# Reordering the turn from the output projection to the experts in a one-core hybrid decoder step

## The reference, cut to what matters

```
x = x + merged @ w_out
xt = rmsnorm(x) * norm2_g
g_logits = xt @ w_rg + b_rg ;  e_logits = xt @ w_rexp + b_rexp
one group of 4 (top 1), then 2 of its 8 experts (top 2), weights w
for e in range(32):
    h = silu(xt @ w_e_gate[e]) * (xt @ w_e_up[e])       # 1024 -> 256
    y = y + combine[:, e:e+1] * (h @ w_e_down[e])       # 256 -> 1024
out = rmsnorm(x + y) * final_norm_g
```

## Time and profile before

| | us |
|---|---|
| median of 3 runs | 782.0 (781.23 to 782.25) |
| the profiled execution's own time | 780.97 |
| its span | 779.2 |
| TensorE busy | 736.3 (94%) |
| VectorE busy | 409.2 (53%) |
| ScalarE busy | 260.4 (33%) |
| data moved | 190.78 MB, mean 245 GB/s |

### The profile page before, as it was taken

How to read it: one execution, slowest core, us unless ns; L and a number is a source line. 1 busy time by engine, 2 the same in 40 slices (tenths; PEclk the granted TensorE clock), 3 DMA queues, 4 the chain that set the end, 5 groups by cost and what they waited for, 6 DMA issues and landing times.

```text
span 779.2 us, 12795 instructions
## 1 busy us (share of the span) xinstructions
PE 736.3 (94%) x5298; PEld 569.7 (73%) x5298; DVE 409.2 (53%) x756; ACT 260.4 (33%) x451; POOL 74.8 (10%) x105
## 2 busy tenths in 40 slices
PE   8999999999999999999999999998899999778784
PEld 6999999999999777899999988884333333323232
DVE  6989839996347685666154286555121121114226
ACT  5652351123476636443243333230111111100113
POOL 0100022001002111000000100011111212111100
PEclk9999999999999999999999999999999999999999
DMA  8578326434338442500251596289999999999994
GB/s 342 204 261 323 109 82 91 132 115 146 110 114 307 161 176 87 214 1 1 109 180 51 186 396 265 89 352 385 416 423 423 418 424 423 421 424 424 422 400 185
DMA packets 38191, 190.78 MB, mean 245 GB/s; under 512 B 5930, under 2 KB 7498, under 8 KB 21912
## 3 DMA queue, kind: packets, MB, share of 16 engines
q1 hardware_dynamic: 23696, 148.22, 48.1%
q0 software_dynamic: 11248, 35.08, 13.4%
q10 hardware_dynamic: 3184, 6.60, 2.3%
HBM read 176.27 MB, written 21.41 MB: 254 GB/s over the span
## 4 chain that ended last, share of the span: by engine, by line
PE 76%; DMA 14%; DVE 5%; ACT 3%; issue 1%; SPq 1%; DVEq 0%; ACTq 0%; POOLq 0%
PE ps L667 72%; DMA sb<-in_wexp 11%; PE ps L681 4%; DMA expert_rows<-sb 2%; DMA sb<-expert_rows 1%; DVE sb L2799 1%; DMA sb<-in_xT 1%; DVE sb L2330 1%; DVE sb L2316 1%; SPq L567 1%; ACT sb L1455 1%; ACT sb L1655 1%; DVE sb L2732 0%; ACT sb L1677 0%; ACT sb L1660 0%
## 5 line engine op out<-in xcount | busy, mean ns | idle before, releaser
L667 PE MATMUL ps<-sr 128*128 128x288 f32 (+3 forms) x2906 | 407.3, 300 | 3.5 <-DVE ps L2737 3.1
L667 PEld LDWEIGHTS ps<-sr 128*128 128x128 f32 (+1 forms) x2906 | 386.7, 188 | 18.9 <-issue 5.8
L667 PE MATMUL ps<-sb 128*64 128x512 f32 (+17 forms) x1994 | 292.5, 427 | 28.6 <-DMA sb<-in_wexp 16.5
L667 PEld LDWEIGHTS ps<-sb 128*64 128x64 f32 (+7 forms) x1994 | 143.1, 146 | 150.5 <-issue 123.4
L2666 DVE SCALAR_TENSOR_TENSOR sb<-sb,ps 128x256 f32<-128x256 f32 x16 | 6.7, 421 | 117.5 <-ACT sb L1860 117.5
L681 PEld LDWEIGHTS ps<-sb 128*128 128x128 f32 (+3 forms) x398 | 42.2, 140 | 32.6 <-issue 30.2
L681 PE MATMUL ps<-sb 128*128 128x128 f32 (+3 forms) x398 | 53.7, 273 | 3.8 <-DVE sb L2669 1.6
L2278 DVE TENSOR_TENSOR sr<-sb,sr 128x2048 fp32r<-128x2048 f32 (+1 forms) x17 | 39.3, 2319 | 29.0 <-ACT sr L1569 19.0
L2674 DVE COPY sb<-ps 128x1024 f32<-128x1024 f32 x15 | 18.4, 1225 | 56.1 <-PE ps L667 56.1
L1455 ACT ACTIVATE sb<-ps 128x576 f32<-128x576 f32 (+4 forms) x33 | 23.2, 704 | 71.8 <-PE ps L667 56.0
L2389 DVE SCALAR_TENSOR_TENSOR sb<-sb,ps 128x576 f32<-128x576 f32 x24 | 18.1, 753 | 46.5 <-PE ps L667 46.3
(11 more groups left out here) (293 smaller groups left out, 499.7 us busy)
## 6 DMA issues: line engine op xcount, KB each, us to landing
sb<-in_wexp SPq DMA_DIRECT2D x91, 1024.0 KB, 21.9
sb<-in_wstream SPq DMA_DIRECT2D x33, 1024.0 KB, 6.1
expert_rows<-sb ACTq DMA_DIRECT2D x1, 4608.0 KB, 24.9
sb<-in_mkT POOLq DMA_DIRECT2D x8, 512.0 KB, 6.9
sb<-in_mv POOLq DMA_DIRECT2D x8, 512.0 KB, 5.1
sb<-expert_rows SPq DMA_DIRECT2D x4, 1024.0 KB, 9.5
sb<-in_wexp SPq DMA_DIRECT2D x5, 768.0 KB, 23.3
sb<-in_x SPq DMA_DIRECT2D x4, 512.0 KB, 14.2
```

The source lines that it names most:

```text
L667: return signed(nc.tensor.matmul(*a, **kw))
```

## The change

It changes the order of work in the turn, not what is computed.

- The `w_out` jobs run as w02, w22, w03, w04, w23, w24. Slots 10 to 13 of the ring now lie on blocks 0 and 1 and are issued when w04 is filled, slot 14 when w23 is, slots 15 to 18 when w24 is.
- Tiles 3 and 4 are turned, squared and multiplied with the router in two column halves (jobs xa and xb; the mean square is made of two sums, the first passed as bias to the root).
- The gain `norm2_g` is no longer in the normalized rows: ScalarE writes them as a scaled copy (`scaled_rows`), and VectorE applies the gain at each pair's turn, in two halves (`rows_turned`, `turned_half`), in place of ScalarE's one copy. VectorE's `norm` and GpSimd's multiply are gone, and so is the load of the gain for all partitions (512 KB).
- The constant of `ranks` carries -2048 on its diagonal, so that one comparison tells both that a row chose an expert and where it goes: `select_first` takes 2 operations on the PSUM result in place of 3 that came behind `place_rows`.
- The second column half of `first_rows(4)` and the expert counts move behind `gate_up(0, 0)`; the 19 small VectorE operations that make numbers and gate weights move behind `rows_turned(1)`, and ScalarE's two Exp behind the first pair's tanh.
- PSUM tiles from w03 on are given by a table written by hand (`plan_pairs`).

```diff
+SLOTS_E += [straight(24320), straight(O_A + 16640)]
+SLOTS_E += w_out_slots(0)
+SLOTS_E += [[(27648, ((1280, 2), (1, 1024)), 0, 2048)]]
+SLOTS_E += w_out_slots(2)
...
-            for n, job in ((8, "w31"), (9, "w22"), (10, "w23")):
+            for n, job in ((8, "w31"), (9, "w22")):
                 filled(sp, job)
                 main_chunk(n)
-            sp.wait_ge(w_used, NBLOCKS - 2)
-            for n in range(11, 15):
+            filled(sp, "w04")
+            for n in range(10, 14):
                 main_chunk(n)
-            sp.wait_ge(w_used, NBLOCKS)
+            filled(sp, "w23")
+            main_chunk(14)
+            filled(sp, "w24")
             for n in range(15, 19):
...
TensorE, from tile 3 on:
+            two_blocks(0, 3, range(5))
+            turn_h("x2T2", 2, all_kts)
+            two_blocks(0, 3, range(5, KT))
+            table(1)
+            logits(2, "x2T2", all_kts)
+            two_blocks(0, 4, range(1))
+            logit_sums(2)
+            two_blocks(0, 4, range(1, 4))
+            turn_h("xa3", 3, low_half)
+            two_blocks(0, 4, range(4, 7))
+            ranks(2)
+            two_blocks(0, 4, range(7, KT))
+            two_blocks(2, 3, range(3))
+            table(2)
+            turn_h("xa4", 4, low_half)
+            two_blocks(2, 3, range(3, 6))
+            logits(3, "xa3", low_half)
+            two_blocks(2, 3, range(6, KT))
+            two_blocks(2, 4, range(2))
+            turn_h("xb3", 3, high_half)
+            two_blocks(2, 4, range(2, 4))
+            logits(3, "xb3", high_half)
+            two_blocks(2, 4, range(4, 5))
+            logit_sums(3)
+            logits(4, "xa4", low_half)
+            two_blocks(2, 4, range(5, KT))
+            first_rows(0, low_half)
+            ranks(3)
+            turn_h("xb4", 4, high_half)
+            first_rows(1, low_half)
+            first_rows(2, range(2))
+            logits(4, "xb4", high_half)
+            first_rows(2, range(2, 4))
+            logit_sums(4)
+            first_rows(3, low_half)
+            first_rows(0, high_half)
+            first_rows(1, high_half)
+            table(3)
+            ranks(4)
+            first_rows(2, high_half)
+            first_rows(4, low_half)
+            table(4)
+            first_rows(3, high_half)
...
                 gate_up(i, 0)
                 if i == 0:
+                    first_rows(4, high_half)
+                    counts()
...
                 gate_up(i, 1)
...
ScalarE:
+            def first_square(t):
+                act.wait_ge(h_ready, first_h(t))
+                square(t, 0, D // 2, R_SA + t)
+                part = at(R_SA + t, (1, 1), pn=WROWS[t])
+                fn(part, part, ACT.Identity, scale=1.0 / D, bias=at(O_EPS, (1, 1), pn=WROWS[t])).then_inc(half_root, 1)
...
+            copy_turned("x2T2", 2, range(KT))
+            first_square(3)
+            copy_logits(2)
+            scaled_rows(2)
+            copy_turned("xa3", 3, low_half)
+            first_square(4)
+            copy_turned("xa4", 4, low_half)
+            for t in (3, 4):
+                second_square(t)
+                copy_turned(f"xb{t}", t, high_half)
+                copy_logits(t)
+                scaled_rows(t)
...
VectorE:
+                filled(dve, f"rk{t}")
+                op(v.tensor_tensor(at(sel, (RB, 2), (1, RB), pn=R), at(R_ROW, (0, 2), (1, RB), pn=R),
+                                   pat(pair(f"rk{t}"), 0, (1, 2), (0, RB), pn=R), ALU.is_equal))
+                c.do(v.tensor_scalar(at(sel, (1, 128), pn=R), at(sel, (1, 128), pn=R), at(R_SS + t, (1, 1), pn=R), None, ALU.mult),
                      sel0_ready)
...
+            def rows_turned(i):
+                dve.wait_ge(xt_ps, i + 1)
+                wait_pos(dve, gu_ps, i)
+                turned_half(PS_X, 0).then_inc(half_sb, 1)
+                turned_half(PS_X, 1).then_inc(xT_sb, 1)
...
+            add_h(0, 4)
+            add_table(2)
+            add_h(2, 3)
+            inverse_norm(3)
+            choose(3)
+            add_h(2, 4)
+            select_first(3)
+            place_rows(3)
             inverse_norm(4)
             choose(4)
+            select_first(4)
+            place_rows(4)
             add_table(3)
-            place_rows(4)
-            select_first(4)
-            first_turned()
+            first_turned(0)
             add_table(4)
             dve.sem_inc(idx_ready, 1)
+            first_turned(1)
...
                 for i in range(i0, i1 - 1):
                     hidden(i)
                     if i == i0:
                         result(i)
+                    rows_turned(i + 1)
+                    if i == 0:
+                        numbers_and_gates()
```

More of the change, by code:

```diff
@@ L37 @@
 NOROW = 4096
+CHOSEN = 2048
 WB = 2048
@@ L283, in plan_jobs @@
     jobs += pieces_at(n + 1)
[L284 to L290, removed]
+    jobs += ["w00", "w20", "w01", "w11", "x2T0", "w21", "lT0", "lg0", "w31"]
+    jobs += ["rk0", "x2T1", "w02", "tb0", "lT1", "lg1", "w22"]
+    jobs += ["rk1", "x2T2", "w03", "tb1", "lT2", "lg2", "xa3", "rk2", "w04"]
+    jobs += ["tb2", "xa4", "w23", "xb3", "lT3", "lg3", "w24"]
+    jobs += ["rk3", "xb4", "lT4", "lg4", "tb3", "rk4", "xs", "tb4", "cnt"]
     return {j: i for i, j in enumerate(jobs)}
@@ L372, with plan_pairs @@
 J = plan_jobs()
-PS_X, PS_GU, PS_H, PS_Y = (J[job] % 4 for job in ("tb4", "rk4", "cnt", "xs2"))
+def plan_pairs():
+    pairs = {job: i % 4 for job, i in J.items() if i <= J["lg2"]}
+    p0, p1, p2, p3 = (pairs[job] for job in ("lT2", "lg2", "w03", "tb1"))
+    assert sorted((p0, p1, p2, p3)) == list(range(4))
+    pairs.update(w04=p2, xa3=p3, rk2=p0, w23=p1, tb2=p0, xa4=p3, lT3=p2, w24=p0, xb3=p1, lg3=p1, lT4=p3)
+    pairs.update(rk3=p1, xb4=p0, xs=p2, lg4=p0, tb3=p1, rk4=p0, tb4=p1, cnt=p3)
+    return pairs
+PAIR = plan_pairs()
+NTH = {job: sum(PAIR[other] == PAIR[job] for other in J if J[other] < J[job]) for job in J}
+TURNED = ["x2T0", "x2T1", "x2T2", "xa3", "xa4", "xb3", "xb4"]
+PS_X, PS_GU, PS_H, PS_Y = (PAIR[job] for job in ("tb4", "rk4", "cnt", "xs"))
 SEEDED = {1: PS_GU, 3: PS_Y, 4: PS_GU}
@@ new lines, in _ @@
+            low_half, high_half = range(4), range(4, KT)
+            all_kts = range(KT)
+            one_block(0)
+            one_block(1)
+            turn_h("x2T0", 0, all_kts)
+            one_block(2)
+            logits(0, "x2T0", all_kts)
+            one_block(3, range(3))
+            logit_sums(0)
+            one_block(3, range(3, KT))
+            two_blocks(0, 2, range(2))
+            ranks(0)
+            two_blocks(0, 2, range(2, 5))
+            turn_h("x2T1", 1, all_kts)
+            two_blocks(0, 2, range(5, KT))
@@ new lines, in _ @@
+            table(0)
+            logits(1, "x2T1", all_kts)
+            two_blocks(2, 2, range(1))
+            logit_sums(1)
+            two_blocks(2, 2, range(1, KT))
+            ranks(1)
+            two_blocks(0, 3, range(5))
[7 more added lines that the diff above has]
+            turn_h("xa3", 3, low_half)
@@ L1314, in body @@
                 gate_up(i, 1)
+                if i == 0:
+                    for ps_ in (PS_X, PS_H, PS_Y):
+                        emptied(ps_)
                 if last:
@@ L1871, in pairs @@
                         hidden_turned(i)
-                    if i < i1 - 1:
-                        rows_turned(i + 1)
+                    if i == 0:
+                        gates()
                 hidden_turned(i1 - 1)
```

342 lines of the change are left out of this document (164 added, 178 removed).

## The result

| | before | after |
|---|---|---|
| median of 22 runs, us | 781.44 | 783.33 |
| lowest and highest, us | 779.6, 783.89 | 781.66, 785.99 |
| ratio, 95% interval | | 1.0020 [1.0012, 1.0029] |
| profiled execution, us (span) | 780.97 (779.2) | 783.52 (781.7) |

The change makes the kernel about 1.6 us slower (0.0020 x 781.4; the medians lie 1.9 us apart), which lies on the bound of 0.2%. I had forecast 782.1 us against 782.0, that is +0.1. The time lies in the whole range, 780.4 to 784.2, but above my forecast's own range of 781.4 to 783.0; the size was wrong by 1.5 us.

The account below looks back on a forecast made before the run. From 557 us the weight stream bounds it, so when it last runs dry decides. Chunk 19 and chunks 22 and 23 allowed -0.2 to +0.6, taken as +0.1: 781.1 us profiled, plus 1.0 gives 782.1; range 780.4 to 784.2.

Parts of the forecast that it names:

- rival 3: Turn: tile 4's chain, `add_h(2, 4)` behind all of `choose(3)`, is late and delays the first pair; 783.9 us, chance 0.15.
- At what time does the weight stream last run dry: Weight stream in the turn: the deciding question; before, it would have run dry at 544.4 us, 1.4 us to spare.
- I credit 0 for it by itself: Early chunks in slots 10 to 13: they fill 3.7 us of idle DMA time but only empty the queue sooner; 0.
- rival 1: Early chunks: the 3.7 us of filled idle DMA time carries through to the end; 778.3 us, chance 0.09.
- rival 2: Turn: rows land 1 to 2 us earlier, `gate_up(0, 1)` no later; 780.6, at most 780.1 us; chance 0.09.
- Plus 0.3 for three more pieces: TensorE before `gate_up(0, 0)`: three more pieces of turns and logits start anew, 0.1 us each, bounds 0 to 0.2.
- The last rows go out about 0.6 us later: ScalarE scales the last rows behind tile 4's logits copy; landing for chunk 19 between 0.4 earlier and 0.6 later.
- I take +0.1, near the middle of what both sides allow: Stream's resumption: the later of chunk 19 and chunks 22 and 23 moves it -0.2 to +0.6 us; taken as +0.1.
- `choose(4)` 524.4 to 524.8: Start of `choose(4)` in the turn: no earlier than its 524.49 before, as its shorter chain begins behind all of `choose(3)`.
- Moving numbers and gates "gives nothing": VectorE's 19 operations, 5.0 us, move from before the first pair's tanh to about 549 to 554 us; cost 0.
- Identity at nothing: ScalarE's new `first_square`: Identity between Square and Sqrt needs no table loads, 0; other bound two loads a tile, 2.56 us.
- The wait of 0.35 us at 499: TensorE waits for the copy of tile 2's logits, as ScalarE has `first_square(3)` ahead of it; plus 0.35 us.

Follow-up runs that it names:

- late_chunks: Changed kernel with chunks 10 to 13 waiting for w23 in place of w04; 785.07 us, ratio 1.0052 to the kernel before.
- merged: Changed kernel with the router's low halves of tiles 3 and 4 multiplied directly ahead of the high ones, two pieces fewer; 783.07 us, ratio 1.0014.
- release: Changed kernel with chunks 22 and 23 issued at the end of `gate_up(0, 1)`, not at the first instruction behind it; 782.47 us, ratio 1.0016.
- scaled_first: Changed kernel with ScalarE scaling tile 4's rows ahead of the copy of its logits; 783.66 us, ratio 1.0024.
- numbers_ahead: Changed kernel with numbers and gates ahead of the first pair again, on VectorE and ScalarE; 784.11 us, ratio 1.0028.
- rows_ahead: Changed kernel with the high half of `first_rows(4)` back ahead of `gate_up(0, 0)`, the counts staying behind it; 782.46 us, ratio 1.0013.
- three_edits: Changed kernel with `first_rows(4)`'s high half ahead of `gate_up(0, 0)`, 22 and 23 issued at `gate_up(0, 1)`'s end, router halves set together; 782.34 us, ratio 1.0001.
- merged_release: Changed kernel with the router's halves set together and chunks 22 and 23 issued at the end of `gate_up(0, 1)`; 782.21 us, ratio 1.0014.

## Why the prediction was right about the mechanism and wrong in size

The number is inside the range partly by luck. The range reached up to 784.2 us for the sake of rival 3, whose cause did not act in the changed kernel (below), and by a sign that I had set myself, "a second dip near 544", the forecast of +0.1 was wrong: the dip came, 342 GB/s at a share of 0.91 from 544 to 546 us.

- **"At what time does the weight stream last run dry"** was the right question. late_chunks shows it with an unchanged TensorE, and from 557 us on the changed kernel streams at 423 GB/s with TensorE idle for 1.04 us of 79, which costs nothing.
- **"I credit 0 for it by itself"**, the early chunks: right as a forecast of the change, since rival 1 and rival 2 did not come. But they are not worthless: without them the changed kernel is 1.7 us slower (stream: 1.7). They help to make up for 15 to 18, which go 1.6 us later than before (520.29 against 518.71). I had moved 15 to 18 back by 1.1 and never priced that.
- **"Plus 0.3 for three more pieces"** is the term that was mis-sized on TensorE's side. merged measures 0.3 us a piece, above the upper bound. 15 to 18 were already 0.5 late, and `gate_up(0, 0)`, which I put at 531.5, began at 538.19 - 2.2 - 3.5 = 532.5 (20 and 21, which its end releases, went at 536.20 against 536.15): the 0.9 us that the reordering was to give did not come. The starts of TensorE's matmuls from `table(1)` (497.07 before, 496.69 after) to `gate_up(0, 0)` say where it went. The way takes 0.43 us longer, where my terms make it 0.92 shorter. The work that left saves 1.2 us. The 72 matmuls of 512 columns on it take 17.35 us before and 18.14 after, the 48 of the logits 2.95 and 3.37, the three sums and four tables 1.63 and 2.06: 1.6 us more for the same matmuls, now in more pieces. The wait at 499 us is 0.34 of that, so the pieces cost 1.3 us in place of 0.3. From there my own arithmetic holds. The added wait, foreseen as 2.15 us, is 2.2: VectorE's second half goes at 537.29 and TensorE begins at 538.19. So `gate_up(0, 1)` was at 538.19 in place of 537.1, and 22 and 23 at 543.66 in place of 542.6. I had written that each us counts from 537.3 on, which gives 0.9. The dip itself, by the windows and by release, costs 0.3 to 0.4.
- **"The last rows go out about 0.6 us later"**: they went out 1.2 us later. GpSimd's issue was at 525.13 before and at 526.32 after, since ScalarE's scaling began at 523.68 and 524.86:

```profile
523.68 1.15 ACT L1841 ACTIVATE sb<-sb 128x1024 f32<-128x1024 f32 x1 [0.18 <-DVE sb L2491]
```

```profile
524.41 0.28 ACT L1539 ACTIVATE sb<-ps 128x128 f32<-128x128 f32 x1 [1.40 <-PE ps L698]
524.86 1.15 ACT L1937 ACTIVATE sb<-sb 128x1024 f32<-128x1024 f32 x1 [0.17 <-ACT sb L1539]
```

  Before, the scaling waited for VectorE's inverse; after, it stands behind the copy of the logits, for which ScalarE was idle for 1.40 us. The landing was 0.8 us shorter (8.0 in place of 8.8 us, GpSimd's issue to chunk 19's), as foreseen of an emptier queue. So chunk 19 was 0.42 us later, inside my -0.4 to +0.6.
- **"I take +0.1, near the middle of what both sides allow"** is the step that failed. The side of 22 and 23: bytes 1.6 us behind the issue at 543.66, at 545.3, against the 544.4 at which the stream was to run dry, +0.9. The side of chunk 19: +0.42. Both have 0.36 more, since this execution ran 0.36 us ahead at the last issue from `in_wstream`: 1.3 and 0.8 us. Both came out late at once, because both hang on the time at which TensorE is done with tile 4 (its logits for the rows, the first pair behind them for 22 and 23); I had taken a middle value as if one could make up for the other. It is also why the single edits bring so little: mend one side, and the other is left (release: 1.5 of delay; scaled_first: 1.2). In bytes of all queues, 13.53 MB had moved between 504.4 and 543 us before and 13.23 after, 0.7 us; the dip from 543 to 547.5 adds 0.36. Another 0.4 us (0.18 MB) is lost at 552 to 557 us, at a share of 0.99 but 365 in place of 400 GB/s; why the engines move less there at nearly the same share I did not find out, and no run tells it. The sum is 1.5 us.
- **"`choose(4)` 524.4 to 524.8"**: it began at 525.32 (rival 3's chain of tile 4, 0.8 late, with the pieces ahead of it). Rival 3 decides "from `gate_up(0, 1)` at 537.3 on" and gives 782.0 + (538.19 - 537.3) = 782.9 for what came, 0.4 below what was measured. So the rival's arithmetic held, but not its cause. VectorE's `choose(3)` ended as w24 was done (15 to 18, which wait for it, went at 520.29), so that `add_h(2, 4)` ran from 520.50 to 521.18 with next to no wait, and TensorE turned tile 4's high half only at 521.74. In merged, where w24 is done 1.05 us sooner behind w04, that chain does hold TensorE up, by 0.3 us.
- **Moving numbers and gates "gives nothing"**: they ran from 550.25 to 555.1 us, ahead of `hidden(1)` at 557.42, as foreseen. But numbers_ahead shows that leaving them where they were would have cost 0.9 us of stream. The cost of 0 held only against the kernel before.
- **Identity at nothing**: right. At 498.44 ScalarE ran the first Identity and the copy behind it with no load between them; the only load in the turn stands at 526.03, ahead of the Exp and tanh as before (524.85 there):

```profile
498.44 0.30 ACT L1918 ACTIVATE sb<-sb 128x1 f32<-128x1 f32 x1
498.64 0.26 ACT L1539 ACTIVATE sb<-ps 128x128 f32<-128x128 f32 x1
526.03 1.28 ACT L1987 ACT_TABLE_LOAD   x1
```

  The Trainium skill, page "ScalarE: Activation LUTs", section "Table sets: the hidden batching unit", has identity in every set; by that rule no load was to be expected, and the trace agrees (none between 470.59 and 526.03 us).
- **The wait of 0.35 us at 499**: right. From the start of the three matmuls of 512 columns ahead of the sum of the logits to the start of the nine behind it TensorE takes 1.28 us (497.96 to 499.24) in place of 0.94 (498.33 to 499.27), 0.34 more.

What stays open: single edits moved the issues nearly as worked out, but their times are not resolved one by one; the part of the loss at 552 to 557 us has no cause yet; and why a piece costs 0.3 us no run tells.

## What to carry to other kernels

Where one saturated stream sets the end, write down every release ahead of it with its time in hand, not only the tightest: an edit that mends one hands the limit to the next, and here three lay within about 2 us (chunk 19, 22 and 23, 24 and 25). Two sides that hang on the same engine's progress are late together: forecast their late ends together, not a middle. Bytes of the queue at a fixed time, set against an event ahead of the change, agreed within 0.1 us in two executions of the same kernel, where 6 to 22 timed runs leave 0.7 to 1.6 us. But they hold what that one execution did: look at its granted clock before an edit gets the credit or the blame.

## What the runs showed of the hardware that I had not expected

In rows_ahead TensorE's granted clock fell for some 4 us behind the idle time ahead of `down(0)`, and `down(0)` took 5.35 in place of 3.65 us. Its windows and the timeline:

```profile
544.00:546.00 2.00, 2.00 (x8) 0.57 (x6) 0.00 (x0) 0.00 (x0) 0.00 (x0) 0.53 1.03 414
546.00:548.00 2.00, 2.00 (x8) 0.63 (x6) 0.00 (x0) 0.00 (x0) 0.00 (x0) 0.62 0.98 414
```

```profile
543.46 5.35 PE L698 MATMUL ps<-sb 128*64 128x512 f32 x16 [0.47 <-ACT sb L1982]
```

A granted clock of 0.53 is near the lower level, 1.2 GHz. three_edits and merged_release show the same in their profiles, merged_release at 544.01:

```profile
544.01 5.35 PE L701 MATMUL ps<-sb 128*64 128x512 f32 x16 [0.47 <-ACT sb L1984]
```

In merged_release TensorE is idle for 0.79, 1.49 and 0.47 us ahead of `gate_up(0, 1)`, `turn_hidden(0)` and `down(0)`; in the changed kernel it is idle for 0.80, 1.49 and 0.47 us at the same places, and the clock stays at 1.00. So idle time just ahead does not decide it; what does is open. It was not free: `down(0)` releases chunks 24 and 25, and all three profiles lose 0.7 to 0.9 us of stream at 547.5 to 552 us against the changed kernel.

The time at which the turn begins differs from one execution to the next, whatever the kernel: the last issue from `in_wstream` lay between 444.31 and 446.86 us in these profiles. This is as large as everything that the edits move. So is what lies behind the stream, where the granted clock differs as well (above). That these two make the intervals wide is likely and not shown. The cause of the first lies ahead of the change and was not looked for.
